# Causal mask of the attention scores: a TensorE product replaced by a VectorE add in PSUM

## The chip, the cores and the metric

The kernel runs on one core of a Trainium2 chip. The metric is the device time of one execution in microseconds (us); lower is better. Three runs of the kernel before took 2565.07, 2565.99 and 2569.24 us.

## What is computed

Two layers of a hybrid trunk over 512 tokens of width 2048. Each layer has six attention heads in two groups (NSA: a compressed, a selected and a window branch), six gated-delta heads, four stick-breaking heads, an output projection and a layer norm. The change touches the selected and the window branch of the attention. With 512 tokens both see every earlier token, so each of the two is a plain causal softmax over its own keys:

```python
ss = einsum(qb, ks) * scale          # selected branch; tok <= t is kept
ps = _masked_softmax(ss, ms, ...)    # where(mask, s, -1e30), minus max, exp, over sum
sw = einsum(qb, kw) * scale          # window branch; dpos >= 0 is kept
pw = _masked_softmax(sw, mw, -1)
out = gb[..., 0:1] * o_c + gb[..., 1:2] * o_s + gb[..., 2:3] * o_w
```

Per layer this is followed by `y @ w_out` and the layer norm. All weights are float32 and are split into a high and a low part for TensorE.

## The kernel before

Each engine has its own program, written out by hand: `@block.tensor`, `@block.scalar`, `@block.vector`, the GpSimd program and `@block.sync`. Engines wait for each other by counting semaphores, and each engine works through its own list in order.

A layer runs two groups of attention (`group(g)`), and a group runs three heads (`for r in range(GROUP)`). There are 12 such heads in the kernel. They are numbered 0 to 11 here in order of time; heads 0, 3, 6 and 9 are the first of their group (`r == 0`). A head has 11 steps (`NSA_STEPS`). TensorE fills each step with products of the next weight tiles (`load_tile`, recorded at L644 to L646, three products for each of 16 k; `nsa_fill` says how many k a step gets), and puts the small work of the attention behind them. A head has eight units `u` of attention, four blocks of 128 queries for each of the two branches: unit `u` has `w = (u % 4 + 1) * 128` keys, so 128, 256, 384, 512, 128, 256, 384, 512. In step `s` TensorE does, in this order:

- the weight products of the step;
- the scores of unit `s - 1` into one of two PSUM banks `SB_` (L925, a float32 product that the trace shows as two instructions), and the mask product (L926), which adds -1e30 above the diagonal to the last 128 columns of the same bank, and whose end counts up `scores`;
- the transposes of the probabilities of unit `s - 2` (L946), which wait for `probs`;
- the product with the values for unit `s - 3` (L954), which waits for `pt_ready`.

VectorE does for unit `u`: wait for `scores`, `reduce` (row maximum in PSUM), a one-column `ts` by -SCALE (`max_ready`), then after ScalarE's exponential a reciprocal of the row sum and a `ts` on the probabilities by that and the gate (`probs`; its tiles are `arena<-arena,tiny,gate_g`). Behind every second unit it does one or two `add_mods` (1024-wide multiply-adds of the modulation weights, `acc<-yT,cact,acc`), and behind unit 7 the rotary embedding of the next head's queries, which TensorE's first product of the next head (L910) waits for. In heads with `r == 0` there are three further pieces: an `add_mods` in unit 0 (not in head 0), a `silu_z` behind unit 0 and an `add_mods` in unit 4 in the first layer.

All of VectorE's calls but a few go through the helper `drained`, so the trace shows them at L1693, each followed by a drain. ScalarE does the exponential from PSUM (L1189), the copy of the transposed probabilities, and the copies of finished weight tiles. GpSimd (POOL) splits the weights: a CAST into `w_hi` and two subtractions into `w_lo` for each half tile (L1629, L1633).

`mask_r` holds the identity and the causal block in float32r. It is filled once at the start by two casts. `C("causal")` is the same block in float32 in the constant tile `cst`; it is 0 on and below the diagonal and -1e30 above.

Of the kernel before, what the change touches and what calls it, by code (L numbers as in the profile page):

```python
# [12 lines left out]
F32R = mybir.dt.float32r  # L13
# [5 lines left out]
P = 128  # L19
# [236 lines left out]
def build(nc, x, positions, c, b_mod, mod0, small_cols, stream, small, lns, const, out, where, layers=DEPTH):  # L256
    x_norm = nc.dram_tensor("x_norm", (TT, P, DM), F32, kind="Internal").ap()
    ctx = ExitStack()
    with ctx:
        def sb(name, shape, dt=F32):  # L260
            return ctx.enter_context(nc.sbuf_tensor(name, shape, dt))
# [9 lines left out]
        w_lo = sb("w_lo", [P, 2, HALF], F32R)  # L271
        acc = sb("acc", [P, DM])
        cst = sb("cst", [P, const.shape[1]])
        mask_r = sb("mask_r", [P, 2, P], F32R)
        rope_cs = sb("rope_cs", [2 * ROPE_HALF, 2, SEQ])
        raw = sb("raw", [P, LOT, TAPS - 1 + SEQ])
        arena = sb("arena", [P, 20, SEQ])
# [21 lines left out]
        def C(name, parts=P):  # L299
            at, n = where[name]  # L300
            return cst[0:parts, at:at + n]
# [8 lines left out]
        ident, ones = C("ident"), C("ones")  # L310
# [11 lines left out]
        PJ, SB_, TB, OB, MB = bank[0:2], bank[2:4], bank[4:6], bank[6], bank[7]  # L322
# [48 lines left out]
        def S(name):  # L371

            if name not in semaphores:
                semaphores[name] = ctx.enter_context(nc.semaphore(name))
            return semaphores[name]
# [23 lines left out]
        def after(name, n):  # L399

            return n + CREDITS.get(name, 0)
# [199 lines left out]
        def _(pe):  # L601
            mm, tr = pe.matmul, pe.transpose
# [53 lines left out]
            def reduce_mod(sums, n):  # L656

                pe.wait_ge(S("mod_sum"), n + FIRST_SUMS)
                for k in range(KT):
                    last = mm(MB[:, k:k + 1], sums[:, k * P:(k + 1) * P], ones[:, 0:1], start=True, stop=True)  # L660
                last.then_inc(S("mod_done"), 1)
# [110 lines left out]
            for l in range(layers):  # L772
# [27 lines left out]
                def group(g):  # L800
# [103 lines left out]
                    for r in range(GROUP):  # L904
                        H = G * GROUP + r
                        q = qT[r % 2]
                        pe.wait_ge(S("roped"), G * 6 + 4 + r)
                        pe.wait_ge(S("exp_done"), after("exp_done", H * 8))
                        for i in range(TT):
                            last = mm(SB_[0][:, i * 32:i * 32 + N_CMP], q[:, i * P:(i + 1) * P],  # L910
                                      cmpb[:, 0, 0:N_CMP], start=True, stop=True)
                        last.then_inc(S("cmp_scores"), 1)
                        for s in range(NSA_STEPS):
                            if l < DEPTH - 1 and r == GROUP - 1 and s == NSA_STEPS - 1:
                                reduce_mod(acc, g + (sums_before[l] + 1))
                            for i, k0, k1 in parts(nsa_fill, s):
                                load_tile(8 + 2 * r + i, k0, k1)
                            if 1 <= s <= 8:
                                u = s - 1
                                i, keys, w = u % TT, (kS, kW)[u // TT], (u % TT + 1) * P  # L920
                                if u == 1:
                                    pe.wait_ge(S("cmp_scored"), H + 1)

                                pe.wait_ge(S("exp_done"), after("exp_done", H * 8 + max(u - 1, 0)))
                                mm(SB_[(u + 1) % 2][:, 0:w], q[:, w - P:w], keys[:, 0:w], start=True, stop=False)  # L925
                                mm(SB_[(u + 1) % 2][:, w - P:w], mask_r[:, 0, :], mask_r[:, 1, :],  # L926
                                   start=False, stop=True).then_inc(S("scores"), 1)
                            if s == 1:
                                pe.wait_ge(S("cmp_probs"), H + 1)
                                pe.wait_ge(S("pt_ready"), after("pt_ready", H * 8))  # L930
                                pe.wait_ge(S("v_ready"), G * 2 + 2)
                                for i in range(TT):
                                    last = tr(TB[0][0:N_CMP, i * P:(i + 1) * P], cmp_p[:, i, :], ident)
                                last.then_inc(S("cmp_pT"), 1)
                            if s == 2:
                                pe.wait_ge(S("cmp_pT_ready"), H + 1)
                                pe.wait_ge(S("y_ready"), after("y_ready", l * 16 + g * GROUP + r))
                                mm(OB[:, :], vcmp[0:N_CMP, :], cmp_pT, start=True, stop=False,
                                   skip_group_check=True)
                            if 2 <= s <= 9:  # L940
                                u = s - 2

                                pe.wait_ge(S("pt_ready"), after("pt_ready", H * 8 + max(u - 1, 0)))
                                pe.wait_ge(S("probs"), H * 8 + u + 1)
                                for j in range(u % TT + 1):
                                    last = tr(TB[(u + 1) % 2][:, j * P:(j + 1) * P],  # L946
                                              prob[u % 2][:, j * P:(j + 1) * P], ident)
                                last.then_inc(S("pt_done"), 1)
                            if 3 <= s <= 10:
                                u = s - 3  # L950
                                i, vals = u % TT, (vS, vW)[u // TT]
                                pe.wait_ge(S("pt_ready"), after("pt_ready", H * 8 + u + 1))
                                for j in range(i + 1):
                                    last = mm(OB[:, i * P:(i + 1) * P], vals[:, j * P:(j + 1) * P],  # L954
                                              probT[u % 2][:, j * P:(j + 1) * P], start=False,
                                              stop=(j == i), skip_group_check=True)
                                last.then_inc(S("pv_done"), 1)
# [731 lines left out]
        def _(dve):  # L1689
            def drained(op):  # L1690
# [7 lines left out]
            tt, ts, stt, cp, reduce, reciprocal, bn_stats, bn_aggr, fill = map(drained, (  # L1698
                dve.tensor_tensor, dve.tensor_scalar, dve.scalar_tensor_tensor, dve.tensor_copy,
                dve.tensor_reduce, dve.reciprocal, dve.bn_stats, dve.bn_aggr, dve.memset))  # L1700
            M, Ad, Su, Mx = ALU.mult, ALU.add, ALU.subtract, ALU.max
# [6 lines left out]
            dve.wait_ge(S("act_ready"), 1)  # L1708
            stt(cact[:, 1, :], cact[:, 0, :], 1.0, cact[:, 1, :], Ad, M)
            ts(cact[:, 1, :], cact[:, 1, :], 0.5, None, M)  # L1710
            cp(mask_r[:, 0, :], ident)
            cp(mask_r[:, 1, :], C("causal"))

            def rope(j_count, x32, n, at):

# [8 lines left out]
            for i in range(2 * KT):  # L1724
                piece, part, rows, k, cols = mod_load(i)
                sums, w = acc0[part][:, cols], 4 * SEQ // rows
# [33 lines left out]
            for l in range(layers):  # L1760
# [48 lines left out]
                def group(g):  # L1809
# [55 lines left out]
                    for r in range(GROUP):  # L1865
                        H = G * GROUP + r
                        for s in range(NSA_STEPS):
                            if s == 0:
# [3 lines left out]
                                scores = SB_[0][:, 0:TT * 32].rearrange("p (t n) -> p t n", t=TT)[:, :, 0:N_CMP]  # L1872
# [13 lines left out]
                            if 1 <= s <= 8:  # L1886
                                u = s - 1
                                i, w, b = u % TT, (u % TT + 1) * P, SB_[(u + 1) % 2]
                                dve.wait_ge(S("scores"), H * 8 + u + 1)
                                reduce(tiny[:, 30:31], b[:, 0:w], AX, Mx)  # L1890
                                ts(tiny[:, u:u + 1], tiny[:, 30:31], -SCALE, None, M).then_inc(S("max_ready"), 1)
                                if r == 0 and u == 0 and not early:
                                    add_mods(l, g, 13)
                                if r == 0 and u == 4:
                                    add_mods(l, g, 16)
                                if s == 1:
                                    dve.wait_ge(S("cmp_pT"), H + 1)
                                    cp(cmp_pT, TB[0][0:N_CMP, :]).then_inc(S("cmp_pT_ready"), 1)
                                dve.wait_ge(S("exp_done"), after("exp_done", H * 8 + u + 1))
                                reciprocal(tiny[:, 31:32], tiny[:, 8 + u:9 + u])  # L1900
                                ts(prob[u % 2][:, 0:w], prob[u % 2][:, 0:w], tiny[:, 31:32],
                                   gate_g[:, i, 3 * r + 1 + u // TT:3 * r + 2 + u // TT], M, M).then_inc(S("probs"), 1)
                                if u % 2:
                                    for j in ((14,), (15,), (17,), (18, 19))[u // 2] if r == 0 else (16 + 4 * r + u // 2,):
                                        add_mods(l, g, j)
                                if has_next and r == GROUP - 1 and u == 7:
                                    dve.sem_inc(S("mod_sum"), 1)
# [399 lines left out]
```

## Time and profile before

| | before |
| --- | --- |
| median of three runs | 2565.99 us |
| span of the profiled execution | 2562.7 us |
| TensorE busy | 2382.4 us, 93% |
| VectorE busy | 1392.5 us, 54% |
| ScalarE busy | 595.4 us, 23% |
| GpSimd busy | 1326.4 us, 52% |
| mask products (L926) | 96 |
| attention heads, in the trace | 230 to 350, 451 to 567, 1469 to 1581, 1677 to 1788 us |

The profile is of one execution. Its span is 3.3 us under the median of the runs. In the timelines below a row has the start in us from the start of the span, the length in us, the engine, the line, the operation with its tiles and shapes, how many instructions are merged in the row, and in brackets how long the engine was idle before it and who ended that. Matmuls overlap, and their ends are modelled, so for TensorE the starts are what counts. In the grouped rows the two numbers after the bar are busy us and mean ns of one instruction, and behind the second bar stands the idle time before them.

### The profile page before, as it was taken

The page shows a single profiled execution, that of the slowest core. Times are in us where ns is not written, and L with a number is a line of the kernel's source. Part 1 is how long each engine was busy: PE and PEld are TensorE (multiplying, and loading weights), DVE is VectorE, ACT ScalarE, POOL GpSimd, SP SyncE. Part 2 cuts the span into 40 slices and gives each one's busy share as a digit, 9 for nine tenths or more (in the row PEclk, how much of TensorE's full clock was granted, in tenths as well). Part 3 has the DMA queues.
Part 4 walks back from the last instruction along what each step waited for, and adds up shares of the span by engine and source line. Part 5 has one row for each costly group of instructions (what it writes and reads, how often), then busy time and mean ns, then how long its engine had stood idle before and what let it go on. Part 6 is the DMA issues. An engine that isn't in the chain of part 4 may idle for free.

```text
span 2562.7 us, 38766 instructions
## 1 busy us (share of the span) xinstructions
PE 2382.4 (93%) x14272; PEld 1896.6 (74%) x14272; DVE 1392.5 (54%) x1992; ACT 595.4 (23%) x1162; POOL 1326.4 (52%) x1018
## 2 busy tenths in 40 slices
PE   0888999998999999999999999999999999999996
PEld 0666777786777777777876877778777777887885
DVE  8965654656555554575135265155656554234536
ACT  0221210222323332232023022022322323224001
POOL 6673457434444445556655644644444444454763
PEclk9998999999999999999999999999999999999998
DMA  9864347322122123454325533532122222222542
GB/s 364 291 229 161 116 161 254 125 85 65 59 67 65 61 67 115 148 192 164 95 73 202 173 109 106 187 115 75 59 67 62 63 67 67 66 80 69 181 140 90
DMA packets 94600, 316.14 MB, mean 123 GB/s; under 512 B 10918, under 2 KB 11174, under 8 KB 93382
## 3 DMA queue, kind: packets, MB, share of 16 engines
q1 hardware_dynamic: 86768, 295.51, 34.1%
q10 hardware_dynamic: 7644, 18.16, 2.0%
q8 instruction: 113, 1.85, 0.3%
q14 instruction: 75, 0.61, 0.1%
HBM read 303.92 MB, written 8.39 MB: 122 GB/s over the span
## 4 chain that ended last, share of the span: by engine, by line
PE 71%; DVE 15%; POOLq 3%; ACT 3%; issue 3%; DMA 2%; POOL 2%; DVEq 1%; ACTq 1%; SPq 0%
PE bank L644 14%; PE bank L646 13%; PE bank L645 13%; DVE arena L1693 11%; PE bank L1159 4%; PE bank L1161 4%; PE bank L1160 4%; DVE acc L1693 3%; PE bank L925 2%; PE bank L954 2%; POOLq L1635 1%; POOL w_lo L1633 1%; ACT arena L1189 1%; PE bank L608 1%; PE bank L946 1%
## 5 line engine op out<-in xcount | busy, mean ns | idle before, releaser
L1629 POOL CAST w_hi<-ring 128x1024 fp32r<-128x1024 f32 (+1 forms) x320 | 363.5, 1136 | 1105.7 <-PE bank L646 922.6
L1633 POOL TENSOR_TENSOR w_lo<-ring,w_hi 128x512 fp32r<-128x512 f32 (+1 forms) x632 | 881.5, 1415 | 48.5 <-issue 1.3
L644 PE MATMUL bank<-h_hi,w_hi 128*128 128x512 f32 x1952 | 827.9, 424 | 14.1 <-POOLq L1635 12.3
L646 PE MATMUL bank<-h_hi,w_lo 128*128 128x512 f32 x1952 | 768.7, 394 | 0.0
L645 PE MATMUL bank<-h_lo,w_hi 128*128 128x512 f32 x1952 | 767.6, 393 | 0.0
L644 PEld LDWEIGHTS bank<-h_hi,w_hi 128*128 128x128 f32 x1952 | 370.6, 190 | 101.1 <-issue 16.4
L646 PEld LDWEIGHTS bank<-h_hi,w_lo 128*128 128x128 f32 x1952 | 369.1, 189 | 83.0
L645 PEld LDWEIGHTS bank<-h_lo,w_hi 128*128 128x128 f32 x1952 | 371.2, 190 | 69.3 <-issue 7.2
L1189 ACT ACTIVATE arena<-bank 128x512 f32<-128x512 f32 (+5 forms) x372 | 173.8, 467 | 737.5 <-PE bank L646 216.6
L1693 DVE SCALAR_TENSOR_TENSOR acc<-yT,cact,acc 128x1024 f32<-128x1024 f32 (+1 forms) x144 | 209.6, 1456 | 37.9 <-DMA acc<-in_b_mod 14.9
L1159 PE MATMUL bank<-w_hi,h_hi 128*128 128x512 f32 x448 | 175.4, 392 | 1.1 <-issue 1.1
L1161 PE MATMUL bank<-w_hi,h_lo 128*128 128x512 f32 x448 | 174.5, 389 | 0.0
L1160 PE MATMUL bank<-w_lo,h_hi 128*128 128x512 f32 x448 | 174.4, 389 | 0.0
L1189 ACT ACTIVATE arena<-arena 128x512 f32<-128x512 f32 (+5 forms) x186 | 95.8, 515 | 198.7 <-DVE arena L1693 169.6
L1693 DVE TENSOR_TENSOR arena<-arena,cst 128x256 f32<-128x256 f32 (+3 forms) x160 | 91.6, 572 | 72.7 <-ACT last_CT L1189 44.9
L1693 DVE SCALAR_TENSOR_TENSOR arena<-arena 128x512 f32<-128x512 f32 (+1 forms) x82 | 94.8, 1156 | 58.0 <-ACT arena L1189 45.4
L1189 ACT ACTIVATE arena<-bank,tiny 128x128 f32<-128x128 f32 (+2 forms) x120 | 67.2, 560 | 246.5 <-DVE tiny L1693 244.2
L1693 DVE SCALAR_TENSOR_TENSOR arena<-raw,conv_h,arena 128x512 f32<-128x512 f32 x108 | 101.9, 944 | 9.0 <-issue 0.4
L1693 DVE TENSOR_TENSOR arena<-bank,yT 128x512 f32<-128x512 f32 x32 | 22.1, 692 | 155.3 <-PE bank L1161 117.9
L1693 DVE TENSOR_TENSOR arena<-arena,rope_cs 32x512 f32<-32x512 f32 (+1 forms) x44 | 38.3, 871 | 113.5 <-DMA arena<-arena 110.9
L1159 PEld LDWEIGHTS bank<-w_hi,h_hi 128*128 128x128 f32 x448 | 84.1, 188 | 20.4 <-issue 3.2
L1160 PEld LDWEIGHTS bank<-w_lo,h_hi 128*128 128x128 f32 x448 | 84.1, 188 | 17.8 <-issue 0.5
(226 smaller groups left out, 2911.7 us busy)
## 6 DMA issues: line engine op xcount, KB each, us to landing
ring<-in_stream SPq DMA_DIRECT2D x352, 512.0 KB, 3.6
yT<-in_stream SPq DMA_DIRECT2D x128, 512.0 KB, 4.5
yT<-in_mod SPq DMA_DIRECT2D x32, 1024.0 KB, 8.2
arena<-in_x ACTq DMA_DIRECT2D x4, 1024.0 KB, 10.3
x_norm<-arena ACTq DMA_DIRECT2D x4, 1024.0 KB, 8.0
arena<-x_norm ACTq DMA_DIRECT2D x4, 1024.0 KB, 9.9
out<-arena SPq DMA_DIRECT2D x3, 1024.0 KB, 3.9
arena<-in_x SPq DMA_DIRECT2D x1, 2048.0 KB, 12.0
```

The costliest lines, as they stand in the source:

```text
L644: mm(PJ[b][:, :], hi, h_hi[:, k, :], start=(k == 0), stop=False)
L645: mm(PJ[b][:, :], hi, h_lo[:, k, :], start=False, stop=False)
L646: last = mm(PJ[b][:, :], lo, h_hi[:, k, :], start=False, stop=(k == KT - 1))
L925: mm(SB_[(u + 1) % 2][:, 0:w], q[:, w - P:w], keys[:, 0:w], start=True, stop=False)
L954: last = mm(OB[:, i * P:(i + 1) * P], vals[:, j * P:(j + 1) * P], probT[u % 2][:, j * P:(j + 1) * P], start=False, stop=(j == i), skip_gro ...
L1159: mm(outs[t][:, :], h_hi[:, k, at], hi, start=(k == 0), stop=False)
L1160: mm(outs[t][:, :], h_hi[:, k, at], lo, start=False, stop=False)
L1161: last = mm(outs[t][:, :], h_lo[:, k, at], hi, start=False, stop=(k == KT - 1))
L1189: made = act.activation(*args, **kw)
L1629: pool.tensor_copy(w_hi[:, par, 0:w], ring[:, slot, 0:w])
L1633: pool.tensor_tensor(w_lo[:, par, at], ring[:, slot, at], w_hi[:, par, at].bitcast(F32), ALU.subtract)
L1693: made = op(*args, **kw)
```

## The change

The mask product and its tile go. The scores product closes its accumulation group itself and counts up `scores`. VectorE adds the causal block to the last 128 columns of the scores in PSUM, in place, between the wait for `scores` and the row maximum. The two casts that filled `mask_r` go too.

```diff
-        mask_r = sb("mask_r", [P, 2, P], F32R)
...
-                                mm(SB_[(u + 1) % 2][:, 0:w], q[:, w - P:w], keys[:, 0:w], start=True, stop=False)
-                                mm(SB_[(u + 1) % 2][:, w - P:w], mask_r[:, 0, :], mask_r[:, 1, :],
-                                   start=False, stop=True).then_inc(S("scores"), 1)
+                                mm(SB_[(u + 1) % 2][:, 0:w], q[:, w - P:w], keys[:, 0:w],
+                                   start=True, stop=True).then_inc(S("scores"), 1)
...
-            cp(mask_r[:, 0, :], ident)
-            cp(mask_r[:, 1, :], C("causal"))
...
                                 dve.wait_ge(S("scores"), H * 8 + u + 1)
+                                tt(b[:, w - P:w], b[:, w - P:w], C("causal"), Ad)
                                 reduce(tiny[:, 30:31], b[:, 0:w], AX, Mx)
```

## Rows read from the trace of the kernel before

**Rows 1.** Page, part 1: busy time, share of the span and instructions by engine

```profile
PE 2382.4 (93%) x14272; PEld 1896.6 (74%) x14272; DVE 1392.5 (54%) x1992; ACT 595.4 (23%) x1162; POOL 1326.4 (52%) x1018
```

**Rows 2.** Groups by shape: mask product, its casts, and VectorE's work behind them

```profile
L926 PE MATMUL bank<-mask_r 128*128 128x128 f32 x96 | 44.6, 465 | 0.0
...
L1693 DVE SCALAR_TENSOR_TENSOR arena<-yT,cact,arena 128x1024 f32<-128x1024 f32 x16 | 26.6, 1662 | 5.4 <-DMA arena<-in_b_mod 3.8 <-DMA yT<-in_mod 0.5
...
L1693 DVE CAST mask_r<-cst 128x128 fp32r<-128x128 f32 x2 | 0.9, 440 | 0.1
```

**Rows 3.** Timeline of TensorE in head 7, units 3 (512 keys) and 4 (128)

```profile
1523.11 1.02 PE L925 MATMUL bank<-arena 128*128 128x512 f32 x2
...
1524.03 0.49 PE L946 MATMUL bank<-cst,arena 128*128 128x128 f32 x3
...
1526.87 0.38 PE L925 MATMUL bank<-arena 128*128 128x128 f32 x2
...
1527.15 0.62 PE L946 MATMUL bank<-cst,arena 128*128 128x128 f32 x4
```

**Rows 4.** Groups by shape on VectorE: 128-column additions and products of two tensors

```profile
L1693 DVE TENSOR_TENSOR arena<-arena,cst 128x128 f32<-128x128 f32 x64 | 37.5, 586 | 15.5 <-ACT arena L1189 11.4
...
L1693 DVE TENSOR_TENSOR arena<-bank,arena 128x128 f32<-128x128 f32 x8 | 2.3, 292 | 0.6
```

**Rows 5.** Timeline of VectorE in head 7, units 3 to 7

```profile
1524.23 0.69 DVE L1693 TENSOR_REDUCE tiny<-bank 128x1 f32<-128x512 f32 x1 [1.20 <-PE bank L926]
...
1526.24 0.64 DVE L1693 TENSOR_SCALAR arena<-arena,tiny,gate_g 128x512 f32<-128x512 f32 x1
...
1528.35 0.29 DVE L1693 TENSOR_REDUCE tiny<-bank 128x1 f32<-128x128 f32 x1
1528.72 0.15 DVE L1693 TENSOR_SCALAR tiny<-tiny 128x1 f32<-128x1 f32 x1
...
1529.64 0.35 DVE L1693 TENSOR_SCALAR arena<-arena,tiny,gate_g 128x128 f32<-128x128 f32 x1
1530.37 0.42 DVE L1693 TENSOR_REDUCE tiny<-bank 128x1 f32<-128x256 f32 x1 [0.38 <-PE bank L926]
...
1533.78 0.56 DVE L1693 TENSOR_REDUCE tiny<-bank 128x1 f32<-128x384 f32 x1
...
1535.55 0.70 DVE L1693 TENSOR_SCALAR arena<-arena,tiny,gate_g 128x384 f32<-128x384 f32 x1
1536.93 0.69 DVE L1693 TENSOR_REDUCE tiny<-bank 128x1 f32<-128x512 f32 x1 [0.68 <-PE bank L926]
...
1538.94 0.55 DVE L1693 TENSOR_SCALAR arena<-arena,tiny,gate_g 128x512 f32<-128x512 f32 x1
```

**Rows 6.** Timeline of TensorE in head 7: transposes of units 4, 6 and 7

```profile
1530.17 0.28 PE L946 MATMUL bank<-cst,arena 128*128 128x128 f32 x1
...
1536.73 0.49 PE L946 MATMUL bank<-cst,arena 128*128 128x128 f32 x3
...
1539.63 0.63 PE L946 MATMUL bank<-cst,arena 128*128 128x128 f32 x4
```

**Rows 7.** Timeline of VectorE in head 6, units 0, 1 and 4

```profile
1479.32 1.34 DVE L1693 TENSOR_SCALAR arena<-arena,tiny,gate_g 128x128 f32<-128x128 f32 x1
...
1481.54 0.42 DVE L1693 TENSOR_REDUCE tiny<-bank 128x1 f32<-128x256 f32 x1
...
1492.04 0.29 DVE L1693 TENSOR_REDUCE tiny<-bank 128x1 f32<-128x128 f32 x1
```

**Rows 8.** Timeline of TensorE in head 6, unit 0

```profile
1480.80 0.30 PE L946 MATMUL bank<-cst,arena 128*128 128x128 f32 x1 [0.52 <-DVE arena L1693]
```

**Rows 9.** Timeline of VectorE in head 6, unit 6

```profile
1498.92 1.55 DVE L1693 TENSOR_SCALAR arena<-arena,tiny,gate_g 128x384 f32<-128x384 f32 x1
```

**Rows 10.** Timeline of GpSimd beside unit 6 of heads 6 and 7

```profile
1497.74 2.52 POOL L1633 TENSOR_TENSOR w_lo<-ring,w_hi 128x512 fp32r<-128x512 f32 x2
...
1534.73 2.64 POOL L1633 TENSOR_TENSOR w_lo<-ring,w_hi 128x512 fp32r<-128x512 f32 x2
```

## The prediction

> **What bounds the kernel now.** The page comes first: TensorE is busy 93% of the span, VectorE 54% [rows 1]. Over the whole kernel TensorE is the bound, and the change takes work from it. But the mask products lie in the 12 attention heads only, and what they are worth is read there. So the second view is the timeline of TensorE and of VectorE in one head, unit by unit, with one question: how long lie the finished probabilities there before TensorE turns them? In head 7 the scaling of unit 7 ends at 1538.94 + 0.55 = 1539.49 [rows 5] and the transposes start at 1539.63 [rows 6], 0.14 us later. In unit 0 of head 6 the scaling ends at 1480.66 [rows 7], the transposes start 0.14 us later as well, and there TensorE is marked idle until VectorE is done [rows 8]. So 0.14 us is the bare handover, and every unit with 0.14 us between the two is one in which TensorE stands and waits for VectorE, also where no idle time is marked, because the ends of matmuls are modelled. What lies above 0.14 us I call slack. The attention heads are a loop between TensorE and VectorE in which VectorE is late in some units of every head.
>
> **What is removed.** The mask product is one of 96 [rows 2]. Its 465 ns is mostly pipeline; what it takes of TensorE is read from starts. Scores plus mask go from 1523.11 to 1524.03 for 512 keys, 0.92 us, and from 1526.87 to 1527.15 for 128 keys, 0.28 us [rows 3]. That is 0.64 us for 384 columns, 1.67 ns a column, so the scores of 128 keys take 0.213 us and the mask is left with 0.28 - 0.213 = 0.067; I take 0.06 us. If nothing else changed, 96 x 0.06 = 5.8 us would go. The scores are also ready 0.06 us earlier. The two casts into `mask_r` (0.9 us) end in a wait for a DMA: the multiply-adds that follow them stand 3.8 us for the bias load [rows 2], which doesn't wait for the casts. I cost them at nothing; if that cover were gone, it would be 0.9 us at most.
>
> **What is added.** One addition of 128 columns on VectorE for each of 96 units, between the scores and the row maximum. No instruction of VectorE writes PSUM in this trace, so the price is bounded. The nearest row is the product of a PSUM and an SBUF tensor of this shape, 292 ns in all 8 [rows 4]. A drain and the issue of the next follow: from 1528.35 to 1528.72, a 0.29 us reduce takes 0.37 us of the engine [rows 5]. So c = 0.38 us. Below, a one-column instruction takes 0.15 us [rows 5], with the drain 0.23, and no 128-column row goes under that. Above, the same shape with both inputs in SBUF has a mean of 586 ns [rows 4], with the drain 0.67, since some are held up by GpSimd. The change's addition has one input in SBUF like the 292 ns row, so I take 0.38. That is 36 us of VectorE's time in the heads. Behind the addition are queued, on VectorE, the maximum and all later work of the head; ScalarE's exponential waits for it, and ScalarE's copies of weight tiles wait behind that. No DMA moves; the modulation loads are freed a little later, with the same lag.
>
> The Trainium skill, SBUF — State Buffer, "Summary: rules for kernel authors", says that a VectorE operation with two SBUF inputs, or in its two-port mode, and a GpSimd operation that reads SBUF block each other in full. By that rule the addition with its PSUM input goes free, as the 292 ns row does, and the sum stays as below; were it held up like the 586 ns row, the sum would be the fourth case below.
>
> **A usual head, walked.** I follow the lag of each engine against the trace of before: P for TensorE, D for VectorE at the end of a unit. In head 7 units 0 to 2 have slack above 0.8 us, so P falls by 0.06 each.
> - Unit 3: VectorE waited 1.20 us for the scores [rows 5], so it starts with them: D = -0.24 + 0.38 = 0.14. The scaling ended at 1526.88 and the transposes came at 1527.15 [rows 3]: slack 0.13. TensorE comes to these transposes with -0.30 and has to wait: P = 0.
> - Unit 4: no wait before its maximum [rows 5], so D = 0.14 + 0.38 = 0.52. The scaling ended at 1529.99, the transposes came at 1530.17 [rows 6]: slack 0.04, P = 0.48.
> - Unit 5: a wait of 0.38, of which 0.09 is the bare issue [rows 5], takes up 0.29: D = 0.23 + 0.38 = 0.61. Slack is 0.8; P = 0.42.
> - Unit 6: no wait: D = 0.99. Slack 1536.73 - 1536.25 - 0.14 = 0.34 [rows 5, 6]: P = 0.65.
> - Unit 7: the wait of 0.68 takes up 0.59: D = 0.40 + 0.38 = 0.78. Slack is 0: P = 0.78.
> The rotary embedding and the next head's first product hang on the end of unit 7 and move with it. So this head is 0.8 us longer, not 0.5 us shorter.
>
> **What GpSimd adds.** In unit 6 the 384-column scaling is issued at 1535.55 while the first of two GpSimd subtractions (1534.73 to about 1536.05) is running, and ends 0.2 us after that one [rows 5, 10]. In head 6 the same scaling is issued at 1498.92, just before the first ends (about 1499.0), loses to the second, and takes 1.55 us, to 0.2 us after the pair's end [rows 9, 10]. With D 0.5 us ahead of P, head 7's scaling comes at about 1536.1 and would lose in the same way: it ends 0.2 us after 1537.37 and moves with GpSimd's own lag of 0.4, near 1538.0, not 1536.25. Then D = 1.75, P = 1.4 behind slack, and unit 7 gives 1.75 - 0.59 + 0.38 = 1.5. Six heads (1, 2, 4, 5, 7, 10) are near this pattern. In heads 8 and 11 the scaling loses already; there the addition of unit 6 hides in the 1 us that it stands, and a slack of 0.2 in unit 7 helps: 0.6 us.
>
> **The first heads of a group.** Here VectorE has more to do and doesn't wait for the scores: the maximum of unit 1 of head 6 and that of unit 4 have no wait before them [rows 7], and the two between are like them. Unit 0 is absorbed, since its scaling stands behind GpSimd for 1.34 us where the shortest of this shape is 0.35 [rows 5, 7]. Units 1 to 4 add in series, 4 x 0.38 = 1.5; units 5 and 6 bring about one more addition and unit 7 another, less 0.2 and what waits remain: 2.0 us. Head 0 has less absorbed, head 3 has a wait of ScalarE's in unit 3 that takes up some; I keep 2.0 for all four.
>
> **The sum.** 6 x 1.5 + 2 x 0.6 + 4 x 2.0 = 18.2 us, with the mask's 0.06 in it already. Without the loss to GpSimd it is 6 x 0.8 + 1.2 + 8.0 = 14. I take 18: the issue lands within 0.1 us of the point where it turns, but on the losing side. Nothing after the heads can take a lag back, since TensorE is the bound there. The span goes from 2562.7 to 2580.7. The median of the runs lies 3.3 us above the profiled span, so 2584 us.
>
> **The rivals.**
> - Hidden: VectorE does the additions in its idle time, and TensorE's 5.8 us come free: 2566 - 6 = 2560 us. For it speaks that VectorE is busy only 54% and has 1 us waits in some units [rows 1, 5]. Against it: the slack that counts is that of units 3, 4 and 7 and of the first heads, and it is 0 to 0.13 us, under c. It decides from c = about 0.2 us downward. 5 in 100. The Trainium skill, Trace Analysis ("Identifying the Most-Contended Engine"), says to ease the engine with the highest occupancy first; read with 93 against 54% that gives this case.
> - Cheap addition: the PSUM write ends early and c is about 0.23: the loop lag shrinks to about 8 us, 2574. 9 in 100.
> - Near nothing: half the lag is taken up in waits that I cost too small (ScalarE's copies, GpSimd holds), and some low-clock stretches of TensorE behind its waits fall away: 2569. 6 in 100.
> - Held-up addition: GpSimd holds it as it holds the two-input rows, c = 0.67: some 40 us, 2605. It decides if the addition's mean is over 0.5 us. 8 in 100.
> - The forecast, VectorE's chain on the path with c near 0.38: 72 in 100, 2577 to 2591 by itself.
>
> **Range and chances.** Cheap and held-up addition are partly taken in: 2573 to 2598. A difference under 0.2% (5.1 us) can't be told from none. Faster is the hidden case, 0.05; same the near-nothing case and a bit of the cheap one, 0.08; slower 0.87.
>
> **What would show it.** An added VectorE row `bank<-bank,cst` 128x128, 96 times, near 292 ns. In a usual head the handover of units 3, 4, 6 and 7 at 0.14 us, and more idle time marked before L946. The 384-column scaling of unit 6 at 1.5 us in head 7 too. Heads 0, 3, 6 and 9 about 2 us longer and the rest of the kernel unchanged. It would be wrong if the addition's row were far from 292 ns, if the scores' handover grew by more than the addition, or if the stretches outside the heads moved.

## The result, and the profile after

The changed kernel takes 2587.36 us (median of 5 runs, 2582.71 to 2590.11), the kernel before 2567.87 us beside it (2565.07 to 2569.53). That is 19.5 us more, a ratio of 1.0076 with a 95% interval of 1.0063 to 1.0090. The profiled execution has a span of 2580.9 us, 18.2 us over that of before, and 2584 was forecast.

The busy times alone tell little of it. The page of the kernel after, part 1, answers to [rows 1]:

```profile
PE 2384.7 (92%) x14176; PEld 1883.1 (73%) x14176; DVE 1432.6 (56%) x2086; ACT 595.7 (23%) x1162; POOL 1326.7 (51%) x1018
```

TensorE has 96 instructions fewer and is no less busy in the sum. VectorE has 96 additions more and two casts fewer, and is busy 40 us longer. Where that goes is in the groups by shape of VectorE, after:

```profile
L1691 DVE TENSOR_SCALAR arena<-arena,tiny,gate_g 128x384 f32<-128x384 f32 x24 | 29.2, 1216 | 1.9
L1691 DVE TENSOR_TENSOR bank<-bank,cst 128x128 f32<-128x128 f32 x96 | 28.8, 300 | 34.3 <-PE bank L924 28.7
```

and the same scaling in the kernel before:

```profile
L1693 DVE TENSOR_SCALAR arena<-arena,tiny,gate_g 128x384 f32<-128x384 f32 x24 | 18.8, 784 | 1.9
```

The addition takes 300 ns (292 was taken from [rows 4]), and none of the 96 takes more. But 10.4 us of the 40 are in another instruction that the change didn't touch: the 384-column scaling went from 784 to 1216 ns. Of its 24, 5 took over 1 us before, and 21 do now: 10 in unit 2 of a head and 11 in unit 6.

TensorE pays for it before the transposes (L946 before, L944 after). The waits of TensorE, kernel before:

```profile
PE bank L910 <- DVE arena L1693: 6.8, 3, 3.0
...
PE bank L946 <- DVE arena L1693: 4.8, 6, 1.5
```

and after (us in all, times, longest):

```profile
PE bank L944 <- DVE arena L1691: 21.9, 26, 1.9
...
PE bank L909 <- DVE arena L1691: 5.9, 2, 3.0
```

The marked waits before the transposes grew by 17.1 us. The start of the next head (L910 before, L909 after), which waits for the rotary embedding, did not get worse: 6.8 us before and 5.9 after.

Head 7, which the prediction walked, after the change. VectorE, units 3 to 7:

```profile
1539.50 0.55 DVE L1691 TENSOR_SCALAR arena<-arena,tiny,gate_g 128x512 f32<-128x512 f32 x1
...
1541.52 0.30 DVE L1691 TENSOR_TENSOR bank<-bank,cst 128x128 f32<-128x128 f32 x1
1541.90 0.29 DVE L1691 TENSOR_REDUCE tiny<-bank 128x1 f32<-128x128 f32 x1
...
1543.18 0.35 DVE L1691 TENSOR_SCALAR arena<-arena,tiny,gate_g 128x128 f32<-128x128 f32 x1
...
1549.55 1.54 DVE L1691 TENSOR_SCALAR arena<-arena,tiny,gate_g 128x384 f32<-128x384 f32 x1
...
1553.56 0.55 DVE L1691 TENSOR_SCALAR arena<-arena,tiny,gate_g 128x512 f32<-128x512 f32 x1
```

TensorE's transposes of units 3, 4, 6 and 7:

```profile
1540.19 0.63 PE L944 MATMUL bank<-cst,arena 128*128 128x128 f32 x4
...
1543.68 0.30 PE L944 MATMUL bank<-cst,arena 128*128 128x128 f32 x1 [0.37 <-ACT arena L1187]
...
1551.23 0.52 PE L944 MATMUL bank<-cst,arena 128*128 128x128 f32 x3 [0.98 <-DVE arena L1691]
...
1554.26 0.63 PE L944 MATMUL bank<-cst,arena 128*128 128x128 f32 x4
```

GpSimd beside unit 6:

```profile
1548.36 2.50 POOL L1631 TENSOR_TENSOR w_lo<-ring,w_hi 128x512 fp32r<-128x512 f32 x2
```

From the addition to the maximum it is 1541.52 to 1541.90, 0.38 us. In all four units the transposes come 0.14 to 0.15 us after the end of the scaling, the bare handover. ScalarE's name in unit 4 is the wait that came last by the record; the scaling ended at 1543.53, 0.15 us before. In unit 6 the scaling was issued at 1549.55, 0.1 us before the end of the first of GpSimd's two subtractions, and stood until 0.23 us after the second.

### The profile page after: what moved, and what is told of

The parts are those of the page before. It is cut to its first block, busy times and chain, and to the rows that moved or that the text cites. A ratio compares the mean times of both kernels' runs of the same rounds, so it can differ in the third digit from the quotient of the medians.

```text
span 2580.9 us, 38762 instructions
## 1 busy us (share of the span) xinstructions
PE 2384.7 (92%) x14176; PEld 1883.1 (73%) x14176; DVE 1432.6 (56%) x2086; ACT 595.7 (23%) x1162; POOL 1326.7 (51%) x1018
## 4 chain that ended last, share of the span: by engine, by line
PE 66%; DVE 19%; ACT 4%; POOLq 3%; issue 3%; DMA 2%; POOL 2%; DVEq 1%; ACTq 1%; SPq 0%
PE bank L643 14%; PE bank L645 13%; PE bank L644 13%; DVE arena L1691 11%; DVE acc L1691 4%; PE bank L1157 4%; PE bank L1158 4%; PE bank L1159 4%; ACT arena L1187 2%; DVE tiny L1691 2%; POOLq L1633 1%; PE bank L607 1%; POOL w_lo L1631 1%; PE bank L952 1%; DVEq L1692 1%
## 5 line engine op out<-in xcount | busy, mean ns | idle before, releaser
L643 PEld LDWEIGHTS bank<-h_hi,w_hi 128*128 128x128 f32 x1952 | 370.1, 190 | 99.5 <-issue 15.8
```

The source lines that it names most:

```text
L643: mm(PJ[b][:, :], hi, h_hi[:, k, :], start=(k == 0), stop=False)
```

## The experiments

All ratios are of runs beside the kernel before on the same chip, and us are that ratio's distance from 1 times 2567.5 us unless the medians are named.

### Each half of the change by itself

`add_beside_product`: the mask product stays, and VectorE adds the causal block as well.

```diff
                                 dve.wait_ge(S("scores"), H * 8 + u + 1)
+                                tt(b[:, w - P:w], b[:, w - P:w], C("causal"), Ad)
                                 reduce(tiny[:, 30:31], b[:, 0:w], AX, Mx)
```

> The mask product stays on TensorE and VectorE adds the causal block a second time. This is the added VectorE work alone, with nothing taken from TensorE. Theory (the addition lengthens the loop between VectorE and TensorE in the attention heads): slower than before by 19 to 23 us, since the 96 times 0.06 us of TensorE no longer come back in the few places where TensorE is late. Rival (the loss in the changed kernel came from the removed product, for example from a later or different handover of the scores): at most 5 us slower.

Measured: 1.0084 (1.0071 to 1.0098), 21.6 us slower. That is within the 19 to 23 us expected. The rival that blamed the removed product or its handover falls: the addition alone brings the whole loss and a little more.

`no_mask`: the product goes and no addition comes, so the scores above the diagonal stay in.

```diff
-                                tt(b[:, w - P:w], b[:, w - P:w], C("causal"), Ad)
```

(against the changed kernel)

> The mask product is gone and nothing adds the mask: the scores above the diagonal stay in. This is the removed TensorE work alone. Theory: 96 times 0.06 us is 5.8 us, of which the units in which TensorE waits for VectorE keep some; 3 to 6 us faster than before. Rival (the scores product as the last of its group hands over later, or TensorE's idle time lowers its clock): no gain, or slower.

Measured: 0.9976 (0.9968 to 0.9985), 6.1 us faster. This is what the removed product is worth, 96 times 0.06 us as read from starts in [rows 3]. The two halves make 21.6 - 6.1 = 15.5 us against 19.5 measured. With the addition in place the product's removal seems to give back 2 us (21.6 against 19.5) and not 6, but each interval is some 3 us wide either way, so that difference is not shown. The waits point that way: where TensorE stands and waits for VectorE, less work before the wait makes the wait longer. TensorE's marked waits before the transposes are 5.9 us in `no_mask`, with no addition, against 4.8 before.

### Which additions cost

The 96 units were cut into three sets that don't overlap, and the change was made in one set at a time. Both engines get the same condition; for `slack_units` it is

```diff
+                                if r > 0 and u in (0, 1):
+                                    tt(b[:, w - P:w], b[:, w - P:w], C("causal"), Ad)
```

with the product kept in the other units; `tight_units` has `r > 0 and u > 1`, `first_heads` has `r == 0`.

> The change is made only in units 0 and 1 of the heads that are not the first of a group: 16 of 96 units, those with more than 1 us of slack. Theory (only additions in units without slack cost): within 1.5 us of before, mean -0.4 us. Rival (every addition costs its share of the whole, whatever its unit): 16/96 of 19 us, 3 us slower.

> The change is made only in units 2 to 7 of the heads that are not the first of a group: 48 of 96 units. Theory: about 10 us slower than before, 1.3 us a head, the sum of the walk through a usual head in the prediction with the hold by GpSimd in unit 6. Without that hold in it the walk gives 0.8 us a head, 6 us. With the slack_units run and a run of the first heads alone the three should add up to the whole change.

> The change is made only in the first head of each group (heads 0, 3, 6 and 9): 32 of 96 units. Theory: 2 to 2.5 us a head, 8 to 10 us slower than before, more an addition than in the other heads, because VectorE has the extra work of the group there and does not wait for the scores. Rival (all heads lose alike): 32/96 of 19 us, 6.5 us.

| run | units changed | ratio | interval | us |
| --- | --- | --- | --- | --- |
| slack_units | 16 | 1.0000 | 0.9992 to 1.0009 | 0 |
| tight_units | 48 | 1.0030 | 1.0019 to 1.0042 | +7.7 |
| first_heads | 32 | 1.0041 | 1.0028 to 1.0054 | +10.5 |
| sum | 96 | | | +18.2 |

The sum is the whole change within its interval. An addition in a unit with over 1 us of slack costs nothing, one in a first head 0.33 us, nearly the 0.38 it occupies VectorE for. The rival of an equal share falls: 16 units would be 3.2 us, outside the interval of `slack_units`. `tight_units` came out under the 10 us expected. Its interval, 5 to 11 us, holds the walk without the hold (6) as well as the one with it (10), so the time doesn't decide between them. Its profile has the hold: 15 of the 24 scalings of 384 columns take over 1 us, where 5 did before.

### Twice the addition

```diff
                                 tt(b[:, w - P:w], b[:, w - P:w], C("causal"), Ad)
+                                tt(b[:, w - P:w], b[:, w - P:w], C("causal"), Ad)
```

> The changed kernel with the addition done twice in each unit, so VectorE's chain is 0.76 us longer a unit than before. Theory: the slack is used up by the first addition, so the second costs more than the first: 40 to 50 us slower than before, 25 us over the changed kernel. The most that it can cost is 96 times 0.38, 36 us over the changed kernel. Rival (a fixed cost of the handover): the second addition is nearly free.

Measured: 1.0206 (1.0191 to 1.0221), 52.9 us over before and 33 over the changed kernel, where 40 to 50 and 25 were expected. The direction is right: the second addition costs more than the first, as there is less slack left. The size has a part that isn't the chain. The table has the length of each group of three heads in the profiled executions, from the first product of its first head to the last product with the values of its third, in us, and in brackets how much of it ran at the lower of TensorE's two clock levels (half the speed):

| heads | before | changed | twice |
| --- | --- | --- | --- |
| 0, 1, 2 | 123.8 (10.7) | 133.4 (16.9) | 146.2 (30.2) |
| 3, 4, 5 | 121.0 (6.8) | 126.5 (5.7) | 137.6 (15.8) |
| 6, 7, 8 | 111.0 (0) | 114.6 (0) | 122.6 (0) |
| 9, 10, 11 | 110.6 (0) | 114.3 (0) | 121.6 (0) |

In heads 6 to 11 the granted clock is 1.00 in all three kernels. There the first addition brings 7.4 us and the second 15.2, 0.15 and 0.32 us for each of the 48. In heads 0 to 5 `add_twice` spends 23.4 us more than the changed kernel at the lower level. If TensorE loses half of such time, an estimate that holds where it never waits and is too high elsewhere, that is 11.7 us. Of the 39.1 us by which the twelve heads are longer than in the changed kernel it leaves 27.4, near the 25 expected. The rival, a second addition that is nearly free, falls.

### The same chain, made shorter

If the chain scores, maximum, exponential, scaling sets these heads, then the kernel before must gain from a shorter one, though nothing about the mask changes. ScalarE scales the queries when it copies them, the maximum is written negated, and the one-column multiplication between them goes:

```diff
-                                reduce(tiny[:, 30:31], b[:, 0:w], AX, Mx)
-                                ts(tiny[:, u:u + 1], tiny[:, 30:31], -SCALE, None, M).then_inc(S("max_ready"), 1)
+                                reduce(tiny[:, u:u + 1], b[:, 0:w], AX, Mx, negate=True).then_inc(S("max_ready"), 1)
...
-                                fn(prob[u % 2][:, 0:w], SB_[(u + 1) % 2][:, 0:w], ACT.Exp, scale=SCALE,
+                                fn(prob[u % 2][:, 0:w], SB_[(u + 1) % 2][:, 0:w], ACT.Exp, scale=1.0,
...
-                                        copy_group(8 + 2 * r, qT[(r + 1) % 2])
+                                        copy_group(8 + 2 * r, qT[(r + 1) % 2], SCALE)
```

`negated_max` is this on the kernel before, `negated_max_add` on the changed one. (`copy_group(6, qT[0])` gets the factor too, and the compressed branch multiplies by 1.0.)

> The kernel before (mask product on TensorE), with VectorE's chain made shorter: the queries are scaled when ScalarE copies them, and the row maximum is written negated, so the one-column multiplication by -SCALE between the maximum and the exponential goes (0.15 us and its drain, 0.24 us, 96 times). Theory: the same chain that the addition lengthens gets shorter, and units 3, 4, 6 and 7 and the first heads have TensorE waiting: 4 to 10 us faster than before. Rival (before, VectorE was never more than just in time, and TensorE did not wait): no gain.

> The changed kernel with the same shortening: the addition comes, the one-column multiplication goes, so the chain is 0.14 us longer a unit than before and TensorE still saves its 0.06 us. Theory: the lag shrinks from 19 us to about 6 us over before, 13 us faster than the changed kernel. Rival (the cost is the addition's traffic in PSUM and not the length of the chain): the changed kernel's loss stays, 15 us or more over before.

Measured: `negated_max` 0.9976 (0.9967 to 0.9986), 6 us faster by the ratio and 5 by the medians (2562.47 against 2567.53). `negated_max_add` 0.9998 (0.9987 to 1.0008), level with before, where 6 us over before was expected. So 0.24 us off each unit takes back 20 us in the changed kernel and 6 in the one before: the same 0.24 us is worth three times as much where the slack is gone. Not all of that need be the shorter chain itself. The scalings of 384 columns that take over 1 us fell from 21 to 10 as well, their mean from 1216 to 881 ns, and no run separates the two. The rival that the addition's own traffic in PSUM costs falls, since the addition is still there in `negated_max_add`, with TensorE's waits before the transposes down from 21.9 us to this:

```profile
PE bank L944 <- DVE arena L1691: 8.9, 15, 1.8
```

The rival of `negated_max`, no gain before the change, falls as well.

### GpSimd's hold on the scaling

```diff
-                for i in range(0, w, SEQ):
-                    at = slice(i, min(i + SEQ, w))
+                for i in range(0, w, SEQ // 2):
+                    at = slice(i, min(i + SEQ // 2, w))
```

`add_short_splits` is this on the changed kernel, `short_splits` on the kernel before, `negated_short_splits` on `negated_max`.

> The changed kernel with GpSimd's subtraction into w_lo cut into four instructions of 256 columns instead of two of 512, so an instruction of GpSimd that holds VectorE's scaling is half as long. Theory (the scaling of unit 6 stands behind a whole GpSimd subtraction, which is 4 us of the lag): the mean of the 384-column scaling falls from 1.22 us to under 1.0, and the kernel is 2 to 5 us faster than the changed one, so 14 to 17 us slower than before. Rival (the hold is not on the path): the scaling gets shorter and the time stays at 19 to 20 us over before. A cost of the cut itself, more instructions on GpSimd, would show in the run of the same cut without the change.

> The kernel before with the same cut of GpSimd's subtractions. It is the base for the run with the change. Theory: within 3 us of before; GpSimd is idle 48% of the span, and the holds of before are in units with slack but for heads 6, 8, 9 and 11.

> The kernel before with the negated maximum and the cut of GpSimd's subtractions together. Theory: the gain of the negated maximum, 5 us, and up to 2 us more; if the cut costs by itself, as much less.

Measured: `short_splits` 1.0004 (0.9996 to 1.0013), `add_short_splits` 1.0049 (1.0034 to 1.0064), 12.6 us over before where the changed kernel is 19.5. The cut by itself costs 1 us or nothing and gives back 7 us where the addition is. In its profile the 384-column scaling is back under its length of before:

```profile
L1691 DVE TENSOR_SCALAR arena<-arena,tiny,gate_g 128x384 f32<-128x384 f32 x24 | 18.1, 755 | 1.9
```

So about a third of the loss is time in which VectorE stood behind GpSimd; with intervals of 3 to 4 us either way on both runs the share is rough. The gain is a little above the 2 to 5 us expected. It comes in spite of a lower clock: four of the six runs of `add_short_splits` had a granted clock of 0.981 or 0.982 and took 2579.8 to 2584.1 us, the two at 0.985 and 0.986 took 2576.4 and 2570.9. Why the clock was lower there is open.

`negated_short_splits`: 0.9969 (0.9958 to 0.9980), 2559.6 us against 2567.85 beside it. It is the fastest of all, 8 us under the kernel before and some 27 under the changed one, and the step over `negated_max` alone, 2 us, is within the two intervals.

## Why the prediction was right

**The bound.** The reading that TensorE stands behind VectorE wherever the handover is 0.14 us held. `first_heads`, `tight_units` and `slack_units` show it unit set by unit set, and `negated_max` shows that it was so before the change.

**What is removed.** 5.8 us was worked out from starts, `no_mask` gives 6.1. It is the worth of the product with no addition beside it.

**What is added.** c = 0.38 us was taken from the 292 ns row with its drain. The row after has 300 ns and the engine is taken 0.38 us: 1541.52 to 1541.90. The write to PSUM costs 8 ns more. Both bounds, 0.23 and 0.67, were far off, and the held-up rival falls: all 96 additions, with one input in PSUM and one in SBUF, took 299 or 300 ns, and 43 of them ran beside an instruction of GpSimd, 20 beside a subtraction. The Trainium skill, SBUF — State Buffer, "Summary: rules for kernel authors", says that of a GpSimd operation that reads SBUF and a VectorE operation that has two SBUF inputs or is in its two-port mode, the second one to issue is fully blocked until the first finishes. The addition has one input in SBUF, and the trace agrees that GpSimd doesn't block it.

**The usual head, walked.** Lags of TensorE in head 7, from the transposes' starts in [rows 3, 6] and those above, less the 13.10 us that the head starts later:

| unit | predicted | measured |
| --- | --- | --- |
| 3 | 0.0 | 1540.19 - 1527.15 - 13.10 = -0.06 |
| 4 | 0.48 | 1543.68 - 1530.17 - 13.10 = 0.41 |
| 6, with the hold | 1.4 | 1551.23 - 1536.73 - 13.10 = 1.40 |
| 7 | 1.5 | 1554.26 - 1539.63 - 13.10 = 1.53 |

Heads 4 and 5 follow the same walk: their transposes of units 4, 6 and 7 lag by 0.4, 1.4 and 1.5 us. In heads 8 and 11 the lag at unit 7 is 0.5, where 0.6 was predicted.

The walk missed two things. In unit 2 the scaling takes 1.03 us now, where it took 0.48: it comes while GpSimd's CAST is running and stands until 0.2 us after it. That takes up the whole slack of unit 2, which was 0.9 us, but no more, and TensorE leaves it without a lag. The other is the end of the head. In the kernel before, VectorE's rotary embedding of head 8 had an instruction of 1.22 us beside a CAST of GpSimd, and TensorE waited for the embedding. After the change that instruction takes 0.68 us: it starts 0.01 us ahead of the CAST, and the CAST is the one that takes longer (1.58 us, where it took 1.04). First products of heads 7 and 8, before, and after:

```profile
1506.86 0.98 PE L910 MATMUL bank<-cmpb,arena 128*128 128x31 f32 x8
...
1544.09 1.08 PE L910 MATMUL bank<-cmpb,arena 128*128 128x31 f32 x8 [0.88 <-DVE arena L1693]
```

```profile
1519.96 0.98 PE L909 MATMUL bank<-cmpb,arena 128*128 128x31 f32 x8
...
1557.82 1.08 PE L909 MATMUL bank<-cmpb,arena 128*128 128x31 f32 x8
```

The 0.88 us wait is gone, so head 7 gives back 0.9 of its 1.5 us.

**Head by head.** The growth of each head, from one head's first product to the next, or to its last product with the values in heads 2, 5, 8 and 11. By this measure heads 2 and 5 of the kernel before end at 353.8 and 571.9 us, some 4 us later than the round figures ahead of the prediction. What TensorE lost at its lower clock level, estimated as half of the time at that level, is taken out. It matters in head 0 (2.5 as read), in head 2 (5.4 as read) and in head 5 (1.0 as read):

| heads | predicted, each | measured |
| --- | --- | --- |
| 1, 2, 4, 5, 7, 10 | 1.5 | 1.7, 2.0, 1.5, 1.5, 0.6, 1.0: sum 8.3 |
| 8, 11 | 0.6 | 0.6, 0.6: sum 1.2 |
| 0, 3, 6, 9 | 2.0 | 2.8, 3.1, 2.5, 2.1: sum 10.5 |
| all | 18.2 | 20.0 |

The mis-sized term is the first heads, 10.5 instead of 8.0. The walk let units 1 to 4 add in series and did not ask what GpSimd does in them. In head 6 after the change:

```profile
1498.37 1.35 DVE L1691 TENSOR_SCALAR arena<-arena,tiny,gate_g 128x384 f32<-128x384 f32 x1
```

```profile
1499.86 0.30 PE L944 MATMUL bank<-cst,arena 128*128 128x128 f32 x1 [1.41 <-DVE arena L1691]
```

That is unit 2: its scaling took 0.48 us before and now runs into a subtraction too, and TensorE waits 1.41 us. The same happens in unit 2 of heads 0, 3 and 9. At unit 4 heads 3, 6 and 9 lag by 1.9 to 2.0 us, where four additions in series make 1.5. Heads 0 and 3 then lose the unit 6 scaling to GpSimd as well (0.70 and 0.69 us before, 1.54 now), which adds 1.1 us to each; the prediction took that loss for the usual heads only. In heads 6 and 9 it was lost before already.

**Outside the heads.** As read, the heads are 22.5 us longer in sum and the span 18.2, so the rest got 4.3 us shorter, where it was forecast that nothing happens. The prediction named such a move as a sign of being wrong. Part of it is the clock: the two profiled executions differ in where TensorE's clock fell. A stretch of the kernel after, with the granted clock as the third number from the end:

```profile
356.00:363.00 7.00, 7.00 (x30) 6.42 (x30) 0.00 (x0) 0.29 (x1) 0.19 (x1) 0.52 0.00 0
```

and of the kernel before, in the output projection of the first layer:

```profile
1060.00:1063.00 3.00, 2.81 (x7) 2.23 (x8) 2.50 (x5) 0.42 (x1) 2.25 (x3) 0.50 0.57 165
```

At the end of head 2 the kernel after runs 6.8 us at the lower level, 1.2 GHz, and loses 3.4 us by the estimate above. The kernel before did not there, and lost time at 1060 us, where the kernel after ran at the full 2.4 GHz. It is not the change that does this. `negated_max`, which keeps the product and has no addition, has the same stretch at the same place, and so have `no_mask` and `first_heads`:

```profile
350.80:357.40 6.60, 6.60 (x22) 5.71 (x22) 0.87 (x2) 0.60 (x1) 2.84 (x3) 0.50 0.01 2
```

By the same estimate the clock makes 2.5 of the 22.5 us in the heads and 1.8 of the 4.3 us outside them. The other 2.5 us are not explained. They don't look like the change's doing either: the kernels `no_mask`, `first_heads`, `negated_max` and `slack_units`, whose changes lie in the heads too, are 4.8, 3.9, 0.3 and 0.0 us shorter than the kernel before outside them. So two spans can differ by up to 5 us where nothing was changed, and the median difference of 19.5 is the better number for the change.

**What was luck.** The walk and its prices held, unit by unit. That its sum, 18.2 us, is the growth of the span to the tenth is luck. The heads grew by 20.0 us with the clock's part taken out: the first heads lost 2.5 us more than predicted, heads 1 and 2 0.7 us more, heads 7 and 10 1.4 us less. The rest of the span happened to be shorter.

**The rivals.** Hidden (2560): its 6 us exist, and `no_mask` has them, but the addition doesn't hide. Cheap and held-up addition fall with the 300 ns row. Near nothing: some waits do give time back, as at head 8, but others grew as much, and in the heads the time at the lower clock level grew from 17.5 to 22.6 us where this rival had it fall. The busy shares of the whole span, 93% against 54%, point at the hidden case, and so do the 74% of TensorE's weight loads; they gave the wrong sign here.

## What to carry over

An engine that is busy half of the time can still be late in some rounds of every loop. Before work is moved to it, read the handover to the bound engine unit by unit, take the smallest gap as the bare latency, and count only what lies above it as slack. Here 16 additions with slack were free and 32 without cost 0.33 us each, so where a mask must go to the engine with more idle time, put it only in the units with slack. It was free there, but it gained nothing either (1.0000). The same reading points the other way as well: one short instruction taken out of that chain was worth as much as the whole product that the change set out to save.

## What was not expected of the hardware

- The change made an instruction that it never touched 55% slower: the 384-column scaling went from 784 to 1216 ns, since it now comes when GpSimd is working. Whether it wins or loses turns on less than 0.4 us of its issue. Issued 0.48 us before the first subtraction ended it took 0.70 us, ahead of the second; issued 0.10 us before that end it stood until 0.2 us after the second, 1.53 to 1.56 us in all; issued 0.25 us into the second, 1.23 or 1.24 us. Cutting GpSimd's instructions in half brought it to 755 ns and the kernel 7 us, though GpSimd then spends longer in the sum. In `short_splits` two 256-column subtractions take 1692 ns where one of 512 took 1422.
- An addition in place in PSUM takes 300 ns for 128 columns, 8 ns more than a product from PSUM into SBUF.
- In heads 0 to 5 TensorE ran 17.5 us at the lower clock level before the change, 22.6 us after it and 46.0 us with the additions doubled; in heads 6 to 11 it was at the full clock in all three. Why the two layers differ is open. Over whole spans the granted clock was 0.983 to 0.986 in the runs of the changed kernel and 0.980 to 0.984 in those of `add_twice`.
